# A hybrid attention and expert block: the first z product in two halves of its contraction, and the order of the loads before it

## What is computed

```python
ada = c @ w_ada + b_ada                       # c: 1 x 1024, w_ada: 1024 x 6144
shift1, scale1, gate1, shift2, scale2, gate2 = split(ada, 6)
h = rms_norm(x, norm1_g) * (1.0 + scale1) + shift1
z = h @ w_in                                  # w_in: 1024 x 1184
# z feeds a sliding-window attention and a latent attention; their output goes through w_out,
x = x + gate1 * mix
h2 = rms_norm(x, norm2_g) * (1.0 + scale2) + shift2
x = x + gate2 * peer_ffn(h2, ...)             # product keys, top 16 of 16384 experts, gathered rows
```

## Time and profile before

| | us |
|---|---|
| median of 3 runs | 1432.2 |
| lowest, highest | 1430.67, 1434.67 |
| span of the profiled execution | 1431.5 |
| TensorE busy in it | 1390.2 |
| VectorE busy | 1207.8 |
| ScalarE busy | 708.0 |
| GpSimd busy | 782.1 |

### The profile page before, as it was taken

The page is one execution under the profiler, slowest core; times in us unless marked ns, Lnnn a source line. Parts: engine busy times, 40 slices in busy tenths (PEclk is TensorE's granted clock), DMA queues, the critical chain, the costliest instruction groups (busy, mean ns, idle before and its releaser), DMA issues.

```text
span 1431.5 us, 23514 instructions
## 1 busy us (share of the span) xinstructions
PE 1390.2 (97%) x8449; PEld 1277.6 (89%) x8449; DVE 1207.8 (84%) x2633; ACT 708.0 (49%) x1315; POOL 782.1 (55%) x466
## 2 busy tenths in 40 slices
PE   6998899999999999999999999999999999999999
PEld 2464566878999999999999999899999999999999
DVE  5756887764989899988998876589999999999997
ACT  1244775233344886478835863344433334433442
POOL 0001000301578877878877778848755648577560
PEclk9899799999999999999999999999999999999999
DMA  9830011354679999999999999999999999999996
GB/s 353 309 113 1 1 60 59 118 191 171 237 255 312 357 329 350 409 386 338 324 399 390 326 343 385 413 348 398 401 390 388 393 398 386 401 399 401 400 401 228
DMA packets 158229, 438.81 MB, mean 307 GB/s; under 512 B 16608, under 2 KB 50720, under 8 KB 156832
## 3 DMA queue, kind: packets, MB, share of 16 engines
q1 hardware_dynamic: 91632, 244.55, 46.8%
q0 software_dynamic: 46080, 167.79, 30.3%
q10 hardware_dynamic: 20400, 24.95, 4.9%
HBM read 390.02 MB, written 47.22 MB: 305 GB/s over the span
## 4 chain that ended last, share of the span: by engine, by line
PE 87%; DMA 3%; DVE 3%; POOL 3%; ACT 2%; issue 1%; SPq 1%; ACTq 0%; DVEq 0%
PE ps L1292 11%; PE ps L1293 11%; PE ps L1291 11%; PE ps L1240 10%; PE ps L1242 10%; PE ps L1241 10%; PE ps L1251 5%; PE ps L985 5%; PE ps L1111 2%; POOL lo L577 2%; PE ps L1082 1%; DMA qkc<-in_w_ada 1%; PE ps L1153 1%; PE ps L1139 1%; PE ps L1150 1%; PE ps L1141 1%
## 5 line engine op out<-in xcount | busy, mean ns | idle before, releaser
L835 ACT ACTIVATE hi<-raw 128x1024 fp32r<-128x1024 f32 x256 | 270.8, 1058 | 214.7 <-DMA raw<-in_v_tiles 148.3
L577 POOL TENSOR_TENSOR lo<-raw,hi 128x1024 fp32r<-128x1024 f32 x123 | 296.3, 2412 | 146.7 <-ACT hi L835 137.3
L1240 PE MATMUL ps<-h2hi,hi 128*128 128x352 f32 x1024 | 336.3, 328 | 5.3 <-POOL lo L577 5.3
L1242 PE MATMUL ps<-h2hi,lo 128*128 128x352 f32 x1024 | 331.5, 324 | 0.0
L1241 PE MATMUL ps<-h2lo,hi 128*128 128x352 f32 x1024 | 331.0, 323 | 0.0
L1292 PE MATMUL ps<-clo,hi 128*128 128x352 f32 x1008 | 324.1, 322 | 0.0
L1293 PE MATMUL ps<-chi,lo 128*128 128x352 f32 x1008 | 324.1, 322 | 0.0
L1291 PE MATMUL ps<-chi,hi 128*128 128x352 f32 x1008 | 324.1, 322 | 0.0
L590 POOL DMA_INDIRECT row_res<-in_v_tiles,E x91 | 175.3, 1926 | 99.5 <-DVE y_tok L1768 65.2
L1240 PEld LDWEIGHTS ps<-h2hi,hi 128*128 128x128 f32 x1024 | 193.8, 189 | 7.5 <-POOL lo L577 7.4
L1241 PEld LDWEIGHTS ps<-h2lo,hi 128*128 128x128 f32 x1024 | 193.5, 189 | 0.0
(11 more groups left out here) (300 smaller groups left out, 2185.2 us busy)
## 6 DMA issues: line engine op xcount, KB each, us to landing
raw<-in_u_tiles SPq DMA_DIRECT2D x128, 512.0 KB
raw<-in_v_tiles SPq DMA_DIRECT2D x128, 512.0 KB
gelus<-act_out ACTq DMA_DIRECT2D x128, 176.0 KB
act_in<-gelus SPq DMA_DIRECT2D x128, 176.0 KB
gates<-stage SPq DMA_DIRECT2D x32, 512.0 KB
gate<-gates SPq DMA_DIRECT2D x32, 512.0 KB
late<-in_w_ada SPq DMA_DIRECT2D x4, 2048.0 KB, 8.1
qkT<-in_w_ada SPq DMA_DIRECT2D x3, 2048.0 KB, 20.5
```

Source lines behind the costliest of these rows:

```text
L577: nc.gpsimd.tensor_tensor(lo[m % 3][:], raw[m % 3][:], hi[m % 3][:].bitcast(F32), ALU.subtract).then_inc(u_lo, 1)
L835: nc.scalar.activation(hi[m % 3][:], raw[m % 3][:], ACT.Copy).then_inc(t_hi, 1)
L1240: nc.tensor.matmul(out, hi[n % 3][:, cols], dense(h2hi, k), start=(k == 0), stop=False)
L1242: last = nc.tensor.matmul(out, lo[n % 3][:, cols], dense(h2hi, k), start=False, stop=(k == KD - 1))
```

## The change

The order of the chunks becomes ada 2, ada 0, in 1, ada 3, ada 1, in 2, in 0; so ada 0 and 1 are the direct ones and ada 3 a prepared one, and the slots of ada 0, ada 3 and in 1 stay as they were. The scale and the shift are computed and applied in two halves, k = 0 to 3 once ada 2 and 0 are there, k = 4 to 7 once ada 3 and 1 are. TensorE does three token tiles of the first four contraction steps of the first z product, then the row of ada 1 and the modulation of ada 3, the fourth tile's first half, the turns of ada 1, and the second halves of the four tiles. `modulation(4)` and `modulation(5)` stand behind all of them and ahead of the second z product. On VectorE the sum of ada 3 and the half sum of ada 1 stand between the two halves of scale and shift; the constants and the later sums follow the second half. The shift's columns are gathered in PSUM bank 6 rather than 3.

```diff
--- before.py
+++ after.py
@@ -320,7 +320,7 @@
         weights_of = {"ada": w_ada, "in": w_in, "out": w_out, "query": peer_w_query}
         chunks, slot, place, uses = [], [], {}, [0] * 6
 
-        for kind, j, at in (("ada", 2, 0), ("ada", 3, 1), ("ada", 0, 3), ("ada", 1, 4), ("in", 1, 2), ("in", 2, 0), ("in", 0, 1),
+        for kind, j, at in (("ada", 2, 0), ("ada", 0, 3), ("in", 1, 2), ("ada", 3, 1), ("ada", 1, 4), ("in", 2, 0), ("in", 0, 1),
                             ("ada", 4, 3), ("ada", 5, 4), ("ada", 8, 3), ("ada", 9, 4), ("out", 0, 2), ("out", 1, 0),
                             ("ada", 6, 5), ("ada", 7, 5), ("query", 0, 2), ("query", 1, 0), ("ada", 10, 5), ("ada", 11, 5)):
             place[kind, j] = len(chunks)
@@ -338,7 +338,7 @@
             return (accs_late if j in (6, 7, 10, 11) else accs)[:, prepared.index(j) % 2, :]
 
         def ada_at(col):
-            return ps[:, 3, col:col + 1] if col < KD else ada_ps[:, col:col + 1]
+            return ps[:, 6, col:col + 1] if col < KD else ada_ps[:, col:col + 1]
 
         def row_ps(j):
             return ps[0:1, 4 + direct.index(j), :]
@@ -639,13 +639,17 @@
             act.wait_ge(const, 1)
             act.wait_ge(ms1, 1)
             nc.scalar.activation(rstd1, ps[:, 6, :], ACT.Sqrt, bias=eps[:], scale=1.0 / D).then_inc(sd1, 1)
-            for j in direct:
+            def copy_row(j):
                 act.wait_ge(ada_row, direct.index(j) + 1)
                 nc.scalar.activation(ada_rows(j)[:, 0:row_cols(j)], row_ps(j)[:, 0:row_cols(j)], ACT.Copy).then_inc(ada_row_sb, 1)
-                if j == direct[0]:
-                    load_small()
-            act.wait_ge(shift_ready, 1)
+
+            copy_row(direct[0])
+            load_small()
             for k in range(KD):
+                if k == KD // 2:
+                    copy_row(direct[1])
+                if k % (KD // 2) == 0:
+                    act.wait_ge(shift_ready, 1 + k // (KD // 2))
                 act.wait_ge(h_scaled, k + 1)
                 nc.scalar.activation(hT[:, k, :], hT[:, k, :], ACT.Identity, bias=ada[:, k:k + 1]).then_inc(h_ready, 1)
             act.dma_start(wuq[:], mla_w_uq.rearrange("(k p) n -> p k n", p=P)).then_inc(up_in, 16)
@@ -962,12 +966,32 @@
                 pe.wait_ge(sq1, k + 1)
                 last = nc.tensor.matmul(ps[:, 6, :], ones[:], hT[:, k, :], start=(k == 0), stop=(k == KD - 1))
             last.then_inc(ms1, 1)
+            modulation(ada_order[0])
             modulation_row(ada_order[1])
-            modulation(ada_order[0])
             modulation_turned(ada_order[1])
+
+            def first_product(tt, half):
+                if (tt, half) == (0, 0):
+                    arrived(place["in", 1])
+                for k in range(half * KD // 2, (half + 1) * KD // 2):
+                    if tt == 0:
+                        pe.wait_ge(h_ready, k + 1)
+                    last = nc.tensor.matmul(ps[:, z_bank(tt), :], hT[:, k, tt * P:(tt + 1) * P], chunk(place["in", 1])[:, k, :],
+                                            start=(k == 0), stop=(k == KD - 1))
+                return last
+
+            for tt in range(TT - 1):
+                first_product(tt, 0)
             modulation_row(ada_order[3])
             modulation(ada_order[2])
+            first_product(TT - 1, 0)
             modulation_turned(ada_order[3])
+            for tt in range(TT):
+                first_product(tt, 1).then_inc(z_ps, 1)
+            modulation(4)
+            modulation(5)
+            pe.wait_ge(z_ps, TT)
+            pe.sem_inc(chunk_used[slot[place["in", 1]][0]], 1)
 
             def z_tile(n, tt):
                 at = place["in", n]
@@ -980,20 +1004,17 @@
                     pe.wait_ge(z_sb, q - 5)
                 cols = chunks[at][3]
                 for k in range(KD):
-                    if q == 0:
-                        pe.wait_ge(h_ready, k + 1)
                     last = nc.tensor.matmul(ps[:, z_bank(q), 0:cols], hT[:, k, tt * P:(tt + 1) * P],
                                             chunk(at)[:, k, 0:cols], start=(k == 0), stop=(k == KD - 1))
                 last.then_inc(z_ps, 1)
-                if q in (2, 3, 6, 8):
-                    modulation({2: 4, 3: 5, 6: 8, 8: 9}[q])
+                if q in (6, 8):
+                    modulation({6: 8, 8: 9}[q])
                 if tt == TT - 1:
                     pe.wait_ge(z_ps, q + 1)
                     pe.sem_inc(chunk_used[slot[at][0]], 1)
 
-            for n in z_order[:2]:
-                for tt in range(TT):
-                    z_tile(n, tt)
+            for tt in range(TT):
+                z_tile(2, tt)
             z_tile(0, 0)
 
             pe.wait_ge(z_sb, 2 * TT)
@@ -1342,15 +1363,14 @@
                 dve.sem_inc(chunk_used[at], 1)
                 dve.sem_inc(acc_done, 1)
 
-            def modulation(piece, chunks_done):
+            def modulation(piece, chunks_done, k0=0, k1=KD):
                 dve.wait_ge(ada_done, chunks_done)
-                cols = slice(piece * KD, (piece + 1) * KD)
-                settled(tt_(ada[:, cols], ps[:, 3, cols] if piece == 0 else ada_ps[:, cols], b_cols[:, cols], ALU.add))
+                cols = slice(piece * KD + k0, piece * KD + k1)
+                settled(tt_(ada[:, cols], ps[:, 6, cols] if piece == 0 else ada_ps[:, cols], b_cols[:, cols], ALU.add))
 
             dve.wait_ge(c_in, 16)
             modulate(prepared[0])
             reverse(rstd1, sd1)
-            modulate(prepared[1])
 
             def modulate_half(j):
 
@@ -1366,17 +1386,27 @@
                                                            in1=sums, op0=ALU.mult, op1=ALU.add))
                 dve.sem_inc(half_done, 1)
 
+            def scale_half(half):
+
+                k0, k1 = half * KD // 2, (half + 1) * KD // 2
+                modulation(1, 1 + 2 * half, k0, k1)
+                settled(nc.vector.scalar_tensor_tensor(out=gs[:, k0:k1], in0=ada[:, KD + k0:KD + k1], scalar=1.0, in1=g1[:, k0:k1],
+                                                       op0=ALU.add, op1=ALU.mult))
+                for k in range(k0, k1):
+                    nc.vector.scalar_tensor_tensor(out=hT[:, k, :], in0=res[:, k, :], scalar=gs[:, k:k + 1], in1=rstd1,
+                                                   op0=ALU.mult, op1=ALU.mult).then_inc(h_scaled, 1)
+
+            def shift_half(half):
+                modulation(0, 2 + 2 * half, half * KD // 2, (half + 1) * KD // 2)
+                dve.sem_inc(shift_ready, 1)
+
+            dve.wait_ge(cols_in, 48)
+            scale_half(0)
+            shift_half(0)
+            modulate(prepared[1])
             modulate_half(direct[1])
-            dve.wait_ge(cols_in, 48)
-            modulation(1, 2)
-            settled(nc.vector.scalar_tensor_tensor(out=gs[:], in0=ada[:, KD:2 * KD], scalar=1.0, in1=g1[:],
-                                                   op0=ALU.add, op1=ALU.mult))
-            for k in range(KD):
-                nc.vector.scalar_tensor_tensor(out=hT[:, k, :], in0=res[:, k, :], scalar=gs[:, k:k + 1], in1=rstd1,
-                                               op0=ALU.mult, op1=ALU.mult).then_inc(h_scaled, 1)
-                if k == 1:
-                    modulation(0, 4)
-                    dve.sem_inc(shift_ready, 1)
+            scale_half(1)
+            shift_half(1)
 
             for f in range(ROPE // 2):
                 last = nc.vector.memset(freq[:, f:f + 1], ROPE_THETA ** (-2.0 * f / ROPE))
```

## The result

| | before | changed |
|---|---|---|
| median, us | 1431.4 (1429.4 to 1434.7, 4 runs) | 1449.7 (1448.2 to 1452.2, 4 runs) |
| span of the profiled execution | 1431.5 | 1446.4 |
| first matmul of the projections | 93.97 | 103.27 |

Timed twice more, it came to 1.0082 [1.0059, 1.0105] and 1.0084 [1.0063, 1.0105], 12 us each.

What follows compares the result with a forecast made beforehand. TensorE was taken to bound the kernel (87% of the chain), VectorE nearly as late. Late sum of chunk 5 +3.4 and low clock +2.5 give +5.9 on a span of 1431.5, 1437.4; median 0.7 above, so 1438 us, range 1433 to 1442.

Steps and rivals of the forecast that it cites:

- step 3: Shift's first half, VectorE add to ScalarE to TensorE: 1.13 us, first z product starts at 32.3, 8.4 us earlier.
- step 7's constants: VectorE after shift_half(1): free at 53.7 instead of 43.94, then the constants take 9.5 us as before.
- it passes through whole: Front end to kernel's end: a delay or gain only shifts TensorE's later products, so +5.9 us stays +5.9.
- Steps 1 and 2: TensorE's start: modulation(ada 2) done at 22.3, row product of chunk 0 at 29.3, turned matmuls at 31.1.
- edits at no cost: Small edits priced at nothing: shift's PSUM bank, split additions, load_small 2.3 us later, third w_in load's wait.
- Steps 4 to 6: TensorE: three half tiles 10.4 us, clock loss 1.7, row product of chunk 1 3.5; through its turned matmuls at 53.5.
- The 1.7: Clock loss in the first z product: half a low stretch at half speed, 1.7 us, ends 0 and 3.1.
- Clock after that wait: Second z product, after TensorE's wait for the sum of chunk 5: low clock costs +2.5 us, ends 0 and 3.4.
- clock holds: Rival: no low stretches in the front end, TensorE 1.6 late, +2.1 overall, 1434.3 us; chance 0.16.
- faster: Rival: VectorE's lateness never binds TensorE; second product starts at 70.7, 2.3 earlier, 1429.9 us; chance 0.08.
- Every gap in full: Rival: each TensorE gap costs a whole low stretch, 3.1 and 3.4; +8.2 to +9.9, 1440 to 1442 us; chance 0.14.
- Its extra: 1.7 us more if the clock already falls in the row product of chunk 0, making +8.2 into +9.9.

Runs made afterwards that it cites:

- pure delays: Kernel before with 13, 16 or 26 unused VectorE multiply-adds ahead of the scale; 1.0063, 1.0075 and 1.0120.
- the constants between: Changed kernel with VectorE's constants moved ahead of scale_half(1) and shift_half(1), behind the half sum of chunk 1; 1.0012 [0.9994, 1.0029] against the kernel before.

## Why the prediction was wrong

Its direction and its mechanism held: VectorE held until `shift_half(1)`, constants and sums late behind it, a wait before `modulation(5)`, a low clock in the product behind. Removing the queue's part removes the loss. The size was off: +6 was forecast and +12 to +18 came, outside the range in each of three timings. In the profiled execution +5.9 was forecast and +14.9 came. Of the 9.0 us missed, 3.4 lie ahead of the projections, in three terms that the sum had too small or at nothing (step 3, step 7's constants, `modulation(5)`), and 5.6 behind them, where the prediction had "it passes through whole". From the profile of the changed kernel:

- *Steps 1 and 2* held: turns of the row start at 29.82 (30.1 forecast).
- *Step 3, with "edits at no cost", failed.* The first product was put at 32.3 and began at 33.87, +1.6. `load_small` was priced by who reads its data, at 53 us. What counts is that ScalarE issues it in order ahead of the shift: the prediction saw the load's consumer and not the issuer's queue. The experiment with the small loads early shows 1.84 of wait less.
- *Steps 4 to 6* held: three half tiles with the clock's loss 12.1 (10.4 + 1.7), row product of chunk 1 3.5, from there to the shift's addition as forecast. The 1.7 was right by luck: it was taken as half of a stretch of 6.83, and the stretch was 3.41 long (33.77 to 37.18) and fell wholly on the product. VectorE was free at 55.2, late by step 3's 1.5.
- *The constants*, put at 9.5 as before: from 55.19 to 65.52 is 10.3, +0.8. Of this 0.6 is in the first sixteen memsets (0.37 of issue between them, and a longer run) and 0.2 the hand-over before them. Why is not known.
- *`modulation(5)`* was priced as at full clock. It waits, so it is the first to run at half: from the sum's end, 77.83, to the product took 2.0 instead of 0.9, +1.1.
- *Clock after that wait*: +2.5 forecast, 9.31 less 6.77 measured. Right, though again by luck: the low stretch was 10.24 long and not 6.83, and half of it passed under the wait and `modulation(5)`.
- Together 1.5 + 0.8 + 1.1 = 3.4, and 5.9 + 3.4 = 9.3 at the projections, as measured.
- *"Passes through whole"*: in the later timings it was short by a little. The changed kernel's +9.6 to +9.8 became 11.8 and 12.0 in time, the pure delays' 7.6, 8.5 and 16.2 became 9.0, 10.7 and 17.2. In the profile after it was short by 5.6: +9.3 is +10.3 at attention's end, +11.4 where the experts start, +14.9 at the end; the two low stretches shown above, each 3.4 longer, can hold at most 1.7 of it each. But this excess does not go with the delay. The kernel before with unused products starts 0.2 late and ends 4.6 late in its profile, the longest of its twelve runs, with a low stretch of 10.24 from 290 us; one kernel that starts 11.4 late (`modulation(5)` later) ends only 9.8 late. So part or all of the 5.6 may be how that execution went; what makes it stays open. So does why the first timing was 5 us above the other two.

Of the rivals, "clock holds" and "faster" fell with the profile. "Every gap in full" came nearest, with +8.2 to +9.9 at the projections against 9.3, but for the wrong reason: neither loss of the clock was as it had it (1.7 and not 3.1, 2.5 and not 3.4), and its 1442 is still below all three timings. Its extra, a fall already in the row product of chunk 0, did come up in three other profiles (8.32 to 8.72 for 7.03).

One reading of the rows was coarse. The prediction put the first fall of the clock behind "one-column matmuls and a wait"; the low stretch began at 29.79, 0.2 us after the one-column matmuls ended, so ahead of nearly all of the wait.

The Trainium skill ("TensorE: Matmul & The Clock Gate", section "HAM oscillation") advises against parting a contraction by waits. The trace agrees that the clock falls behind the gaps; but the price of the split was VectorE's queue. With the constants between, the split kernel loses 1.4 and 1.7 us to the clock, where the kernel before loses 2.6 and 3.1, and takes the same time.

## What to carry to other kernels

When a step is split so that its second half waits for another engine, look in the list of each engine that takes part for independent work behind the new wait, and put that work ahead of it: here one such move was worth about 10 us (1.0012 for 1.0084). Count the gain of an early start as idle time and low clock removed on the bounding engine, not as the shift of the start. An issue of a load is work of the engine that issues it.

## What the runs showed of the hardware

- An issue of a load on ScalarE took 0.33 to 0.48 us, eight of them 3.7, and held the activation behind them (33.01 instead of 31.2, an estimate from the shift columns' 31.07).
- Matmuls of one column, though TensorE is busy with them, stood ahead of most falls of the clock, mostly with a wait; in the kernel before the first fall, at 29.79, came when TensorE had not waited since 20.64 and its last 2 us were such matmuls. Eight or sixteen of them between long products did not bring the clock down (71.32 to 73.03 with the constants between). Six products of 128x512 in a wait of 5.3 us kept it. Eight matmuls of one column took 0.95 to 1.05 at full and 1.87 at half clock.
- Low stretches of the front end were 3.4, 6.8 or 10.2 us long, and 13.7 and 20.5 where TensorE waited 10.40 and 19.55 (13 and 26 added operations). Where one fell varied between runs of kernels that were the same up to there, and moved 1.3 to 1.7 us from one product to the next.
- With eight small loads (0.5 MB in all) issued early, a 2 MB chunk issued ahead of them landed 2.0 to 3.6 us later, in four profiles (33.1 to 34.7 for 31.1).
